# Two preparations of a two-block network: order of the weight splits around the running sums, and place of a narrow tanh

## The chip, the cores and the metric

One Trainium2 chip, one core. The metric is the device time of one execution in microseconds (us), as the median of several executions.

## The reference

The reference runs two blocks one behind the other on 256 tokens of width 1024, in float32. The first block has two layers of hybrid attention with an MLP and is not touched by the change. The second block has two layers, too, each of the form below. What matters here is the third branch, a recurrence of the RWKV-7 kind.

```python
h = rms_norm_2(x, norm_g) * (1.0 + scale) + shift
proj = h @ w_in      # pool, retention and rwkv branches, gates
...
p = p + (p_prev - p) * shift_mu                  # the mix
r, wl, k, v, al = jnp.split(p, split_pts, axis=-1)
w = -jax.nn.softplus(-(w0 + jnp.tanh(wl) @ w2)) - 0.5
decay = jnp.exp(-jnp.exp(w))
a = jax.nn.sigmoid(a0 + al @ a2)
kk = heads(k * k_k)
kk = kk / jnp.maximum(jnp.sqrt(jnp.sum(kk * kk, -1, keepdims=True)), 1e-12)
k = k * (1.0 + (a - 1.0) * k_a)
...
S = S * w_t + sa * b_t + v_t * k_t               # step by step over the tokens
```

The kernel does the recurrence in chunks of 128 tokens, so it needs the logarithms of the decays, summed along the tokens ("running sums"), and their exponentials.

## The kernel before, in words

**Engines.** The program of each engine is written out by hand, in order: `tensor_program`, `vector_program`, `scalar_program`, `gpsimd_program` and `sync_program` (which issues the loads). They meet through one semaphore per engine: `at["name", l]` is the step of VectorE, ScalarE or GpSimd that a waiting engine needs in layer `l`, and `done[...]` a step of TensorE. An engine that waits holds up all that stands behind in its program.

**Weight pieces.** The weights come in pieces of 128 x 2048 float32 (1 MB), in the order of the list `SECOND`: rw6 (half as wide), rw0 to rw5, rq0, rq1, rk0, rk1, u0, u1, rv0, rv1, rg0 and so on. The load of piece n waits until the low half of piece n - 3 has been made (ring of three). ScalarE rounds a piece to its high part in two instructions (`split_to`, printed under L2290, "part0h<-ring"; the piece before must be finished on TensorE but one, as there are two sets of parts). VectorE then makes the low part, raw minus high, in two instructions (L1284, "part0l<-ring,part0h"); GpSimd does so for some other pieces. TensorE multiplies each piece in three products (high x high, high x low, low x high), 48 instructions of 256 columns (L532). Pieces alternate between part0 and part1: rq1, rk1, u1 and rv1 use the same set in one layer, rq0, rk0, u0 and rv0 the other.

**Jobs.** `Jobs.fill()` takes the next job off a list that is the same for every engine: rq0, rq1, rk0, rk1, u0, u1, rv0, rv1, rg0, ... On TensorE a job multiplies its piece. On VectorE the job of a piece splits the low part of the piece after it (`use` goes one ahead), so the job rk1 on VectorE is the split of u0. On ScalarE it splits the high part of the next piece, then copies the job's own result out of PSUM ("Z<-ps"), which waits for the last product. On GpSimd the job rk1 also runs `rotate` (L2882 to L2888), 24 instructions: the rotation of rq, which waits for the copies of rq0 and rq1, then that of rk, which waits for those of rk0 and rk1.

**The stage.** `prepare(l, jobs)` opens each layer. TensorE multiplies rw6 and rw0 to rw5; each is copied out by ScalarE into `praw` and mixed by VectorE (L2009, L2013). Then TensorE goes on in this order:

```python
        jobs.fill()                  # rq0
        ...                          # lw, aa: 8 products "ps<-Z,v2b", need tanh(wa)
        for _ in range(4):
            jobs.fill()              # rq1, rk0, rk1, u0
        ...                          # ksum: 4 products "ps<-kt_,cg", need M.kt = bt ** 2
        jobs.fill()                  # u1
        ...                          # kn: products of the key norms, need n8
        jobs.fill()                  # rv0
        jobs.fill()                  # rv1
        ...                          # transposes of v4, then of bt and kt
```

Around this, ScalarE takes the tanh of `wa` (64 x 256, the narrow one), of `lw` and `aa`; VectorE scales `lw` (L2019), forms the running sums `cu` in eight instructions (L2024), the sum `sS` and the middle values (L2029 to L2032), subtracts them (L2035, step "cm"), multiplies r by the exponential that ScalarE makes of it (L2039, "ar r", waits for "e+"), and scales the keys into `bt` (L2042, step "kk"). ScalarE squares these into `kt` ("kk2"), which TensorE sums over each head ("ksum"). Then come the maximum, root and reciprocal of the norms (L2045, L2048), the difference of the running sums (L2051), and the products into AR, bt and kt (L2055 to L2068), the last of which waits for GpSimd's update of k4 (L2930, L2933).

The change touches `prepare` of `vector_program` and `prepare` of `scalar_program`. Tiles are printed by their buffers: gates is lw, cu, r4, k4 and others; bt_ is bt; kt_ is kt; sc is sS and the middle values; Z holds wa, ee, n8, and the copies of rq, rk, u and rv.

Of the kernel before, what the change touches and what calls it, by code (L numbers as in the profile page):

```python
# [11 lines left out]
ACT = mybir.ActivationFunctionType  # L12
# [65 lines left out]
PIECE = {(l, key): n for n, (l, key, width) in enumerate(PLAN)}  # L78
# [370 lines left out]
def jobs2():  # L449

    names = [f"{n}{j}" for n in ("rq", "rk", "u", "rv", "rg", "pg", "wg") for j in range(2)]
    first = [[n] for n in names]
    halves = [f"h{b}_{j}.{m}" for b in range(3) for j in range(4) for m in range(2)]
    bw = [f"bw{b}_{hf}.{m}" for b in range(2) for hf in range(2) for m in range(2)]
    first += [halves[0:2]] + [[n] for n in halves[2:14]] + [halves[14:16]]
    return first + [halves[16:18]] + [[n] for n in halves[18:24] + ["pr"] + bw[0:5]] + [bw[5:7], bw[7:8]]
# [812 lines left out]
def vector_program(w, K):  # L1269
    e, M, V, ps, at, done = w.e, K.mem, K.vector, K.psum, K.at, K.done  # L1270
# [722 lines left out]
    def prepare(l, jobs):  # L1993
        Z = M.Z[l]
# [26 lines left out]
        for c in range(4):  # L2021
            for i in range(2):
                n_ = slice(i * 128, (i + 1) * 128)
                e.tensor_tensor_scan(cu[:, c, n_], ui[:, 128:256], lw[:, c, n_], 0.0, ALU.mult, ALU.add).then_inc(*V())  # L2024
        jobs.fill()
        cu8 = cu.rearrange("p c (i n) -> p c i n", i=2)
        sS, mid = sc2[:, 36:40], sc2[:, 40:48]
        w.wait_ge(*V.now())
# [4 lines left out]
        w.wait_ge(*V.now())  # L2033
        cu_f = cu.rearrange("p c (i n) -> p (c i) n", i=2)
        e.tensor_tensor(cu_f, cu_f, mid.unsqueeze(2).to_broadcast([128, 8, 128]), ALU.subtract).then_inc(*V("cm", l))  # L2035
        ar_a, ar_r = M.AR[:, :, :, 0, :], M.AR[:, :, :, 1, :]
        spl = lambda t: t.rearrange("p c (i n) -> p c i n", i=2)
        w.wait_ge(*at["e+", l])
        e.tensor_tensor(ar_r, spl(r4), spl(ee), ALU.mult).then_inc(*V("ar r", l))  # L2039
        jobs.fill()  # L2040
        for c in range(4):
            e.tensor_scalar(bt[:, c, :], k4[:, c, :], second_vectors(l, "kk")[:, c:c + 1], None, ALU.mult).then_inc(*V("kk", l))  # L2042
        jobs.fill()
# [2 lines left out]
        ps.free(("ksum", l), V.now())  # L2046
        w.wait_ge(*at["n8 root", l])
        e.reciprocal(Z.n8, Z.n8).then_inc(*V("n8", l))  # L2048
        jobs.fill()
        w.wait_ge(*V.now())  # L2050
        e.tensor_tensor(lw, cu, lw, ALU.subtract).then_inc(*V("lw in", l))  # L2051
        for cp in range(2):
# [59 lines left out]
        for cp in range(2):  # L2112
            t = bank("yT", cp, l)
            for m in range(2):
                c = 2 * cp + m
# [133 lines left out]
    for l in range(L):  # L2249
        jobs = Jobs(jobs2(), lambda name: job2(l, name))  # L2250
# [30 lines left out]
def scalar_program(w, K):  # L2281
    e, M, S, ps, at, done = w.e, K.mem, K.scalar, K.psum, K.at, K.done
# [3 lines left out]
    def act(o, a, f, **k):  # L2286
        return e.activation(o, a, f, **k)  # L2287

    def copy(o, a):
        return e.activation(o, a, ACT.Copy)  # L2290

    def split_to(n):
        while state["split"] <= min(n, len(PLAN) - 1):
            m = state["split"]
            state["split"] += 1
            raw, hi, c = K.raw(m), K.part(m)[0], PLAN[m][2] // 2
            w.wait_ge(*at["piece", m])
            if m >= SPLIT:
                w.wait_ge(*done["piece", m - SPLIT])
            for h in range(2):  # L2300
                copy(hi[:, h * c:h * c + c], raw[:, h * c:h * c + c]).then_inc(*S("hi", m, h))
# [282 lines left out]
    def enter(b):  # L2584

        split_to(PIECE[b, "rw6"])
        squares(b, 0)
        scale_rows(b, 0)
        split_to(PIECE[b, "rw0"])
        modulate(b, 0)  # L2590
        squares(b, 1)
        high_of(b, 0, 0)
        scale_rows(b, 1)
        high_of(b, 0, 1)
        modulate(b, 1)
        for q in range(2):
            high_of(b, 1, q)
# [46 lines left out]
    def prepare(l, jobs):  # L2644
        Z = M.Z[l]
        S.mark("s", "begin", l)
        enter(l)
        c_ = M.cst[:, l, :]
        begins("begin", l)
        mixed = ("mixed", -1, l)  # L2650
        for j in (6, 0, 1, 2, 3, 4, 5):
            nch = 2 if j < 6 else 1
            use(l, f"rw{j}")
            t = bank(("rw", j), l)
            w.wait_ge(*at[mixed])
            copy(Z.praw[:, 0:nch, 1:257], v(t[:, :], c=2, n=256)[:, 0:nch, :]).then_inc(*S("praw", j, l))
            ps.free((("rw", j), l), S.now())
            mixed = ("mix", j, l)
        jobs.fill()
        w.wait_ge(*at["mix", 6, l])  # L2660
        act(Z.wa[0:64, :], Z.wa[0:64, :], ACT.Tanh).then_inc(*S("wl", l))
        for cp in range(2):
            for n, dst, hb in (("lw", M.lw, c_[:, 24:28]), ("aa", M.aa, c_[:, 28:32])):
                t = bank(n, cp, l)
                for m in range(2):
                    c = 2 * cp + m
                    act(dst[:, c, :], t[:, m * 256:(m + 1) * 256], ACT.Tanh, scale=0.5, bias=hb[:, c:c + 1]).then_inc(
                        *S("tanh " + n, cp, l))
                ps.free((n, cp, l), S.now())
        jobs.fill()  # L2670
        jobs.fill()
        sS, ee = M.sc2[:, 36:40], Z.ee
        w.wait_ge(*at["sS in", l])
        act(sS, sS, ACT.Exp).then_inc(*S("sS", l))
        w.wait_ge(*at["cm", l])
        act(ee, M.cu, ACT.Exp).then_inc(*S("e+", l))
        jobs.fill()
        w.wait_ge(*at["kk", l])
        act(M.kt, M.bt, ACT.Square).then_inc(*S("kk2", l))
        jobs.fill()  # L2680
        w.wait_ge(*at["n8 in", l])
        act(Z.n8, Z.n8, ACT.Sqrt).then_inc(*S("n8 root", l))
        jobs.fill()
        w.wait_ge(*at["lw in", l])
        act(M.lw, M.lw, ACT.Exp).then_inc(*S("e lw", l))
        jobs.fill()
        w.wait_ge(*at["ar r", l])
        act(ee, M.cu, ACT.Exp, scale=-1.0).then_inc(*S("e-", l))
        jobs.fill()
        S.mark("s", "ph2", l)  # L2690
        for i in range(2):
            copy(M.vN[:, i, :], bank("vN", i, l)[:, :]).then_inc(*S("vN", i, l))
            ps.free(("vN", i, l), S.now())
        for n, dst in (("bN", M.bN), ("kN", M.kN)):
            copy(dst, bank(n, l)[:, :]).then_inc(*S(n, l))
            ps.free((n, l), S.now())
        jobs.fill()
        jobs.need("u1")
        begins("ph2", l)
        copy(Z.dT[:, 0:2, :], v(bank("pool", 0, l)[:, :], c=2, n=256)).then_inc(*S("dT", 0, l))  # L2700
        ps.free(("pool", 0, l), S.now())
        for i in range(2):
            copy(Z.qTr[:, :, i * 128:(i + 1) * 128], v(bank("qT", i, l)[:, :], h=4, n=128)).then_inc(*S("qT", i, l))
            ps.free(("qT", i, l), S.now())
        jobs.fill()
        jobs.fill()
        w.wait_ge(*at["rot", l])
        for hf in range(2):
            copy(M.grow[:, hf * 512:(hf + 1) * 512], bank("grow", hf, l)[:, :]).then_inc(*S("grow", l))
            ps.free(("grow", hf, l), S.now())  # L2710
        jobs.need("rv1")
        jobs.fill()
        jobs.fill()
        jobs.need("rg0", "rg1", "pg0", "pg1")
        S.mark("s", "ph3", l)
# [6 lines left out]
    for l in range(L):  # L2722
        lnw = V2N * l + V2O["lnw"][0]
        jobs = Jobs(jobs2(), lambda name: job2(l, name))
# [551 lines left out]
```

## Time and profile before

| | |
|---|---|
| median of 3 runs | 1742.17 us (1741.64 to 1742.19) |
| profiled execution, its own time | 1739.01 us |
| its span, first to last instruction | 1737.2 us |
| mean granted TensorE clock | 0.993 |
| busy: TensorE / VectorE / ScalarE / GpSimd | 96% / 58% / 41% / 36% |
| preparation up to the transposes of bt and kt, layer 0 | 1011.8 to 1110.9 us |
| the same stretch of layer 1 | 1378.9 to about 1476 us |

All durations in the document come from one profiled execution, 1739.01 us long, of which the span is 1737.2 us; the runs without a profile took some 3 us more. "Idle before" in a row of the timeline is the time that the engine stood still ahead of the instruction, with the engine and line that released it. A matmul's printed duration (0.28 us) is longer than its share of the time, as matmuls overlap; starts of successive ones are 0.12 us apart at the full clock of 2.4 GHz.

### The profile page before, as it was taken

To read this page: it belongs to the slowest core of one execution; us is meant where nothing else is said; L and a number is where in the kernel's file an instruction comes from. 1 tells how busy PE (TensorE), PEld (TensorE's weight loads), DVE (VectorE), ACT (ScalarE), POOL (GpSimd) and SP (SyncE) were. 2 spreads that over 40 slices of the span, in tenths; PEclk is the share of its full clock that TensorE was granted. 3 is DMA by queue.
4 is the path that set the end of the run, shared out by engine and by line. 5 is a ranking of instruction groups with operands and counts; after the bars stand their busy time and mean duration, and the time that the engine had idled before them with its cause. 6 is when DMAs were issued, how large, how long until landed. Compare 5 with 4: busy or idle time off the path is not lost.

```text
span 1737.2 us, 34448 instructions
## 1 busy us (share of the span) xinstructions
PE 1673.1 (96%) x15214; PEld 1534.2 (88%) x15214; DVE 1008.5 (58%) x1612; ACT 718.8 (41%) x1120; POOL 628.0 (36%) x510
## 2 busy tenths in 40 slices
PE   9999999999999999999999998999999999999997
PEld 8878988899988888987999888999998898999986
DVE  4265366777763454476777876663345668653346
ACT  4434534545344444444444444533222444332223
POOL 1744683000307635733000414225544207144541
PEclk9999999999999999999999999999999999999999
DMA  8422444777545323465775544433223444432322
GB/s 344 148 81 90 137 162 201 274 283 265 178 173 187 123 75 118 142 258 202 271 279 201 175 170 146 159 122 123 99 98 122 144 154 146 153 123 98 123 74 109
DMA packets 44148, 283.57 MB, mean 163 GB/s; under 512 B 5160, under 2 KB 5288, under 8 KB 14176
## 3 DMA queue, kind: packets, MB, share of 16 engines
q1 hardware_dynamic: 42336, 272.23, 44.1%
q0 software_dynamic: 1664, 9.15, 1.4%
q8 instruction: 119, 1.95, 0.5%
q14 instruction: 29, 0.24, 0.0%
HBM read 280.30 MB, written 1.06 MB: 162 GB/s over the span
## 4 chain that ended last, share of the span: by engine, by line
PE 81%; DVE 9%; POOL 5%; ACT 4%; issue 1%; DMA 0%; SPq 0%; POOLq 0%; ACTq 0%; DVEq 0%
PE ps L532 78%; PE ps L540 2%; POOL part0l L2765 2%; POOL part1l L2765 2%; ACT Xh L2290 1%; DVE Xl L1299 1%; DVE part1l L1284 1%; DVE gates L2024 1%; DVE part0l L1284 1%; ACT part1h L2290 1%; ACT part0h L2290 0%; DMA hid<-in_xT 0%; ACT gates L2287 0%; POOL x L2800 0%; ACT raw L2287 0%
## 5 line engine op out<-in xcount | busy, mean ns | idle before, releaser
L2290 ACT ACTIVATE part0h<-ring 128x1024 fp32r<-128x1024 f32 (+2 forms) x218 | 216.3, 1041 | 264.2 <-PE ps L532 256.9
L532 PE MATMUL ps<-Xh,part0h 128*128 128x256 f32 x1080 | 314.9, 292 | 6.0 <-DVE Xl L1299 4.2
L2290 ACT ACTIVATE part1h<-ring 128x1024 fp32r<-128x1024 f32 x218 | 216.3, 1040 | 238.4 <-PE ps L532 236.8
L532 PE MATMUL ps<-Xl,part0h 128*128 128x256 f32 x1080 | 307.5, 285 | 0.0
L532 PE MATMUL ps<-Xh,part0l 128*128 128x256 f32 x1080 | 307.3, 285 | 0.0
L532 PE MATMUL ps<-Xh,part1h 128*128 128x256 f32 x984 | 285.2, 290 | 3.0 <-DVE Xl L1932 1.8
L2765 POOL TENSOR_TENSOR part1l<-ring,part1h 128x512 fp32r<-128x512 f32 x178 | 231.7, 1335 | 152.4 <-ACT part1h L2290 152.4
L2765 POOL TENSOR_TENSOR part0l<-ring,part0h 128x512 fp32r<-128x512 f32 x170 | 224.7, 1355 | 167.8 <-ACT part0h L2290 167.8
L532 PE MATMUL ps<-Xl,part1h 128*128 128x256 f32 x984 | 278.7, 283 | 0.0
L532 PE MATMUL ps<-Xh,part1l 128*128 128x256 f32 x984 | 278.5, 283 | 0.0
L532 PEld LDWEIGHTS ps<-Xh,part0h 128*128 128x128 f32 x1080 | 208.8, 193 | 15.8 <-issue 6.3
L532 PEld LDWEIGHTS ps<-Xl,part0h 128*128 128x128 f32 x1080 | 208.8, 193 | 0.3
L532 PEld LDWEIGHTS ps<-Xh,part0l 128*128 128x128 f32 x1080 | 208.9, 193 | 0.0
L1284 DVE TENSOR_TENSOR part0l<-ring,part0h 128x1024 fp32r<-128x1024 f32 (+1 forms) x132 | 165.9, 1296 | 62.5 <-ACT part0h L2290 62.2
L532 PEld LDWEIGHTS ps<-Xh,part1h 128*128 128x128 f32 x984 | 188.9, 192 | 10.2 <-issue 6.3
L1284 DVE TENSOR_TENSOR part1l<-ring,part1h 128x1024 fp32r<-128x1024 f32 x128 | 155.2, 1254 | 62.0 <-ACT part1h L2290 62.0
L532 PEld LDWEIGHTS ps<-Xl,part1h 128*128 128x128 f32 x984 | 189.0, 192 | 0.1
L532 PEld LDWEIGHTS ps<-Xh,part1l 128*128 128x128 f32 x984 | 188.9, 192 | 0.0
L2800 POOL TENSOR_TENSOR x<-xh,rows 128x512 f32<-128x512 f32 x20 | 33.5, 1673 | 335.8 <-DVE hid L1811 290.8
L532 PE MATMUL ps<-part1h,Xh 128*128 128x256 f32 (+2 forms) x304 | 95.7, 315 | 8.1 <-DVE part1l L1284 3.9
L532 PE MATMUL ps<-Z 64*64 64x64 f32 (+2 forms) x2256 | 98.5, 224 | 0.0
L532 PEld LDWEIGHTS ps<-Z 64*64 64x64 f32 (+1 forms) x2256 | 88.8, 136 | 8.0 <-issue 1.0
(410 smaller groups left out, 3319.2 us busy)
## 6 DMA issues: line engine op xcount, KB each, us to landing
ring<-in_w SPq DMA_DIRECT2D x214, 1024.0 KB, 4.9
hid<-in_ada SPq DMA_DIRECT2D x36, 512.0 KB, 6.5
hid<-in_w SPq DMA_DIRECT2D x6, 1024.0 KB, 11.0
rows<-in_lnrow POOLq DMA_DIRECT2D x6, 1024.0 KB, 7.2
fqk<-in_ada SPq DMA_DIRECT2D x6, 512.0 KB, 6.1
cq<-in_ada SPq DMA_DIRECT2D x6, 512.0 KB, 6.2
gates<-in_c SPq DMA_DIRECT2D x2, 1536.0 KB, 6.4
plain<-in_w SPq DMA_DIRECT2D x2, 1024.0 KB, 7.6
```

What stands on the lines that cost most here:

```text
L532: return e.matmul(o, a, b, start=st, stop=sp)
L540: return e.transpose(o, a, ident[0:a.shape[0], 0:a.shape[0]])
L1284: e.tensor_tensor(lo[:, h * c:h * c + c], raw[:, h * c:h * c + c], f32(hi[:, h * c:h * c + c]), ALU.subtract).then_inc(*V("low", m, h))
L1299: return e.tensor_tensor(hl[1], raw, f32(hl[0]), ALU.subtract).then_inc(*V(*name))
L2024: e.tensor_tensor_scan(cu[:, c, n_], ui[:, 128:256], lw[:, c, n_], 0.0, ALU.mult, ALU.add).then_inc(*V())
L2290: return e.activation(o, a, ACT.Copy)
L2765: e.tensor_tensor(lo[:, o], raw[:, o], f32(hi[:, o]), ALU.subtract).then_inc(*G("low", m, h))
L2800: e.tensor_tensor(x3[:, i, c], xh3[:, i, c], M.rows[:, c], ALU.mult).then_inc(*G())
```

## The change

- VectorE's job rk0 (the split of rk1) moves into the loop of running sums, behind the fourth of the eight; another job, rk1 (the split of u0), stands behind the eighth.
- VectorE's next job, u0 (the split of u1), stands behind the subtraction L2035 and ahead of the wait for "e+". The jobs that stood behind "ar r" and behind the reciprocal are gone; that behind the key scaling is now u1 (the split of rv0). The job behind "ar a" is rv0, as before.
- ScalarE takes the narrow tanh in the loop over the wide pieces, behind the copy of rw1 (j == 1), and no longer behind the job rq0.
- ScalarE does three jobs (rq1, rk0, rk1) ahead of the exponentials, and then the high half of u1. Behind the exponential of cu it does the job u0 and the high half of rv0, ahead of the squares. The squares, the root and the two other exponentials follow each other; the jobs u1, rv0 and rv1 come behind them.
- TensorE's, GpSimd's and the load program are unchanged, and so is what is computed.

```diff
--- before.py
+++ after.py
@@ -2022,7 +2022,8 @@
             for i in range(2):
                 n_ = slice(i * 128, (i + 1) * 128)
                 e.tensor_tensor_scan(cu[:, c, n_], ui[:, 128:256], lw[:, c, n_], 0.0, ALU.mult, ALU.add).then_inc(*V())
-        jobs.fill()
+            if c % 2:
+                jobs.fill()
         cu8 = cu.rearrange("p c (i n) -> p c i n", i=2)
         sS, mid = sc2[:, 36:40], sc2[:, 40:48]
         w.wait_ge(*V.now())
@@ -2033,11 +2034,11 @@
         w.wait_ge(*V.now())
         cu_f = cu.rearrange("p c (i n) -> p (c i) n", i=2)
         e.tensor_tensor(cu_f, cu_f, mid.unsqueeze(2).to_broadcast([128, 8, 128]), ALU.subtract).then_inc(*V("cm", l))
+        jobs.fill()
         ar_a, ar_r = M.AR[:, :, :, 0, :], M.AR[:, :, :, 1, :]
         spl = lambda t: t.rearrange("p c (i n) -> p c i n", i=2)
         w.wait_ge(*at["e+", l])
         e.tensor_tensor(ar_r, spl(r4), spl(ee), ALU.mult).then_inc(*V("ar r", l))
-        jobs.fill()
         for c in range(4):
             e.tensor_scalar(bt[:, c, :], k4[:, c, :], second_vectors(l, "kk")[:, c:c + 1], None, ALU.mult).then_inc(*V("kk", l))
         jobs.fill()
@@ -2046,7 +2047,6 @@
         ps.free(("ksum", l), V.now())
         w.wait_ge(*at["n8 root", l])
         e.reciprocal(Z.n8, Z.n8).then_inc(*V("n8", l))
-        jobs.fill()
         w.wait_ge(*V.now())
         e.tensor_tensor(lw, cu, lw, ALU.subtract).then_inc(*V("lw in", l))
         for cp in range(2):
@@ -2656,9 +2656,10 @@
             copy(Z.praw[:, 0:nch, 1:257], v(t[:, :], c=2, n=256)[:, 0:nch, :]).then_inc(*S("praw", j, l))
             ps.free((("rw", j), l), S.now())
             mixed = ("mix", j, l)
-        jobs.fill()
-        w.wait_ge(*at["mix", 6, l])
-        act(Z.wa[0:64, :], Z.wa[0:64, :], ACT.Tanh).then_inc(*S("wl", l))
+            if j == 1:
+                w.wait_ge(*at["mix", 6, l])
+                act(Z.wa[0:64, :], Z.wa[0:64, :], ACT.Tanh).then_inc(*S("wl", l))
+        jobs.fill()
         for cp in range(2):
             for n, dst, hb in (("lw", M.lw, c_[:, 24:28]), ("aa", M.aa, c_[:, 28:32])):
                 t = bank(n, cp, l)
@@ -2667,26 +2668,26 @@
                     act(dst[:, c, :], t[:, m * 256:(m + 1) * 256], ACT.Tanh, scale=0.5, bias=hb[:, c:c + 1]).then_inc(
                         *S("tanh " + n, cp, l))
                 ps.free((n, cp, l), S.now())
-        jobs.fill()
-        jobs.fill()
+        for _ in range(3):
+            jobs.fill()
+        split_to(PIECE[l, "u1"])
         sS, ee = M.sc2[:, 36:40], Z.ee
         w.wait_ge(*at["sS in", l])
         act(sS, sS, ACT.Exp).then_inc(*S("sS", l))
         w.wait_ge(*at["cm", l])
         act(ee, M.cu, ACT.Exp).then_inc(*S("e+", l))
         jobs.fill()
+        split_to(PIECE[l, "rv0"])
         w.wait_ge(*at["kk", l])
         act(M.kt, M.bt, ACT.Square).then_inc(*S("kk2", l))
-        jobs.fill()
         w.wait_ge(*at["n8 in", l])
         act(Z.n8, Z.n8, ACT.Sqrt).then_inc(*S("n8 root", l))
-        jobs.fill()
         w.wait_ge(*at["lw in", l])
         act(M.lw, M.lw, ACT.Exp).then_inc(*S("e lw", l))
-        jobs.fill()
         w.wait_ge(*at["ar r", l])
         act(ee, M.cu, ACT.Exp, scale=-1.0).then_inc(*S("e-", l))
-        jobs.fill()
+        for _ in range(3):
+            jobs.fill()
         S.mark("s", "ph2", l)
         for i in range(2):
             copy(M.vN[:, i, :], bank("vN", i, l)[:, :]).then_inc(*S("vN", i, l))
```

## Rows read from the trace of the kernel before

**Rows 1.** The page: busy time, share of the span and instructions of each engine.
```profile
PE 1673.1 (96%) x15214; PEld 1534.2 (88%) x15214; DVE 1008.5 (58%) x1612; ACT 718.8 (41%) x1120; POOL 628.0 (36%) x510
```

**Rows 2.** The page: chain that ended last, by engine.
```profile
PE 81%; DVE 9%; POOL 5%; ACT 4%; issue 1%; DMA 0%; SPq 0%; POOLq 0%; ACTq 0%; DVEq 0%
```

**Rows 3.** Timeline, TensorE, layer 0: start, duration, engine, line, operation, count, idle.
```profile
1011.82 0.36 PE L532 MATMUL ps<-Xh,part0h 128*128 128x256 f32 x1 [1.18 <-DVE Xl L1299]
...
1056.33 2.00 PE L532 MATMUL ps<-Z,v2b 64*128 64x256 f32 x16 [1.08 <-ACT Z L2287]
...
1071.84 0.39 PE L532 MATMUL ps<-part0h,Xh 128*128 128x256 f32 x1 [1.82 <-DVE part0l L1284]
...
1080.18 0.39 PE L532 MATMUL ps<-part1h,Xh 128*128 128x256 f32 x1 [2.10 <-DVE part1l L1284]
...
1087.59 1.89 PE L532 MATMUL ps<-kt_,cg 128*8 128x256 f32 x8
...
1110.86 0.22 PE L532 MATMUL ps<-cg,bt_ 64*64 64x64 f32 x1
```

**Rows 4.** Timeline, TensorE, layer 1.
```profile
1378.93 0.35 PE L532 MATMUL ps<-Xh,part1h 128*128 128x256 f32 x1 [1.19 <-DVE Xl L1299]
...
1438.91 0.38 PE L532 MATMUL ps<-part1h,Xh 128*128 128x256 f32 x1 [1.80 <-DVE part1l L1284]
...
1447.23 0.39 PE L532 MATMUL ps<-part0h,Xh 128*128 128x256 f32 x1 [0.82 <-DVE part0l L1284]
...
1453.17 1.89 PE L532 MATMUL ps<-kt_,cg 128*8 128x256 f32 x8
```

**Rows 5.** Windows: stretch, sum, busy PE, PEld, DVE, ACT, POOL; granted clock, DMA share, GB/s.
```profile
582.50:586.00 3.50, 0.00 (x0) 0.00 (x0) 3.30 (x12) 0.67 (x2) 2.74 (x3) 1.00 0.23 37
...
586.50:590.00 3.50, 3.50 (x19) 3.37 (x18) 1.04 (x3) 2.13 (x10) 0.00 (x0) 0.52 0.55 232
...
1081.50:1085.00 3.50, 3.50 (x19) 3.50 (x18) 2.74 (x4) 0.73 (x1) 3.42 (x6) 0.51 0.79 243
```

**Rows 6.** Timeline, VectorE, layer 0.
```profile
1061.52 2.37 DVE L1284 TENSOR_TENSOR part1l<-ring,part1h 128x1024 fp32r<-128x1024 f32 x2 [7.47 <-ACT part1h L2290]
...
1064.53 5.66 DVE L2024 TENSOR_TENSOR_SCAN gates<-cg,gates 128x128 f32<-128x128 f32 x8
1070.11 3.35 DVE L1284 TENSOR_TENSOR part0l<-ring,part0h 128x1024 fp32r<-128x1024 f32 x2
...
1074.88 1.76 DVE L2035 TENSOR_TENSOR gates<-gates,sc 128x1024 f32<-128x1024 f32 x1
1077.77 1.23 DVE L2039 TENSOR_TENSOR AR<-gates,Z 128x1024 f32<-128x1024 f32 x1 [1.12 <-ACT Z L2287]
1078.91 2.35 DVE L1284 TENSOR_TENSOR part1l<-ring,part1h 128x1024 fp32r<-128x1024 f32 x2
1081.18 3.06 DVE L2042 TENSOR_SCALAR bt_<-gates,v 128x256 f32<-128x256 f32 x4
...
1109.07 1.23 DVE L2068 TENSOR_TENSOR kt_<-gates,Z 128x1024 f32<-128x1024 f32 x1 [2.95 <-POOL gates L2933]
...
1123.92 1.14 DVE L2082 TENSOR_SCALAR gates<-gates,v 128x256 f32<-128x256 f32 x4
```

**Rows 7.** Timeline, ScalarE, layer 0: the squares, a split, a copy out.
```profile
1084.27 1.06 ACT L2287 ACTIVATE kt_<-bt_ 128x1024 f32<-128x1024 f32 x1 [4.16 <-DVE bt_ L2042]
1085.24 1.99 ACT L2290 ACTIVATE part0h<-ring 128x1024 fp32r<-128x1024 f32 x2
1087.70 0.60 ACT L2290 ACTIVATE Z<-ps 128x512 f32<-128x512 f32 x1 [0.47 <-PE ps L532]
```

**Rows 8.** Timeline, GpSimd, layer 0: three instructions of the rotation.
```profile
1070.67 1.71 POOL L2884 TENSOR_TENSOR grow<-Z,cs 128x256 f32<-128x256 f32 x1
...
1080.24 1.62 POOL L2882 TENSOR_TENSOR grow<-Z,cs 128x256 f32<-128x256 f32 x1 [3.00 <-ACT Z L2290]
...
1091.27 0.73 POOL L2888 TENSOR_TENSOR Z<-grow 128x256 f32<-128x256 f32 x1
```

## The prediction

> **What bounds the kernel now.** I first read the busy times of the engines: TensorE is busy for 96% of the span and the next engine, VectorE, for 58% [rows 1]. The chain that ended last runs 81% on TensorE and 9% on VectorE [rows 2]. So a split, an exponential or a copy costs time only where TensorE stands and waits for it. I therefore read TensorE's own timeline in the second block's preparation, once for each layer, and looked for idle time ahead of an instruction. Layer 0 has three such places [rows 3]: 1.08 us ahead of the small products of the decay weights (released by the narrow tanh on ScalarE), 1.82 us ahead of rk1 and 2.10 us ahead of u0 (both released by the low half that VectorE splits off). Layer 1 has 1.08 us at the first place too (its row repeats that of layer 0), then 1.80 us ahead of rk1 and 0.82 us ahead of u0 [rows 4]. After these waits the granted clock falls to half: 0.51 over 3.5 us in layer 0 [rows 5]. What that costs is seen on the piece in which it falls. An undisturbed piece runs from 1447.23 to 1453.17, 5.94 us [rows 4]; u0 in layer 0 took 1080.18 to 1087.59, 7.41 us [rows 3]; rk1 in layer 1 took 1438.91 to 1447.23 - 0.82 = 1446.41, 7.50 us [rows 4]. That is 1.5 us lost in each layer. All that the change could win here is 2 x 1.08 + 1.82 + 2.10 + 1.80 + 0.82 + 2 x 1.5 = 11.7 us.
>
> Next I followed what TensorE needs right behind u0: the key sums ("ksum", the products of kt_). They need the squares on ScalarE, these need the four scalings of the keys on VectorE (L2042), and these stand behind everything that VectorE does from the split of rk0 on. VectorE's timeline [rows 6] shows this run from 1061.52 to 1081.18 + 3.06 = 1084.24, 22.72 us with one gap of 1.12 us (for the first exponential). The squares follow at 1084.27, for 1.06 us [rows 7]. The key sums began at 1087.59 in layer 0, only 2.3 us after them. In layer 1 they began 1453.17 - 1378.93 = 74.24 us behind the layer's first wide product, against 1087.59 - 1011.82 = 75.77 us in layer 0 [rows 3, 4]; VectorE's run lies at the same distance in both layers, so there the squares were ready just 0.8 us before TensorE. **Two chains are nearly in step here: TensorE's pieces and VectorE's run to the key scaling. The change shortens the first by much and the second hardly.**
>
> **Part 1, the narrow tanh behind rw1.** It goes where ScalarE otherwise waits for TensorE, so it costs nothing there; its input is ready since the first mix. ScalarE's table stays the same, as no load stands before the tanh now. The products start when rq0 is done, 1055.30 instead of 1056.33: all behind them shifts by -1.03 us, in both layers.
>
> **Part 2, the split of rk1 between the two halves of the running sums.** The eight sums take 1070.11 - 1064.53 = 5.58 us [rows 6], so the split starts some 2.8 us earlier, at 1060.49 + (1064.53 - 1061.52) + 2.79 = 1066.3, and its first half is done by 1068.0. TensorE is free for rk1 at 1071.84 - 1.82 - 1.03 = 1069.0: the wait of 1.82 us (1.80) goes. The split of u0 comes right behind the other four sums, from 1072.4; its first half is ready at about 1074.1, and TensorE comes to it at 1074.8: the wait of 2.10 us (0.82) goes as well, with little to spare. TensorE is then through with u0 at about 1080.6 instead of 1087.6. ScalarE makes the high halves in time: it splits each piece right behind the copy of the one before.
>
> **Part 3, what VectorE does until the keys are scaled.** The run of 22.72 us keeps all its work. The gap of 1.12 us is filled by the split of u1, which is now ahead of the wait for the exponential: two instructions, 2.35 us when alone, 3.35 us beside GpSimd [rows 6]. GpSimd's rotation is why the second price matters. One of its instructions takes 1.71 us beside such a split and it starts on rk only when rk1 is copied out, at 1080.24 [rows 8]. rk1 is now copied at about 1075, so the rotation (12 instructions, about 12 us) runs on without a gap, across the split of u0, the split of u1, the product "ar r" and the key scaling. Before, u0's split (2.35) and "ar r" (1.23) had lain where GpSimd was idle. No row shows "ar r" beside GpSimd; the subtraction of the same size, L2035, took 1.76 us beside it, so "ar r" is bounded by 1.23 and 1.76. The key scaling already costs 3.06 us beside GpSimd, against 1.14 us for the same shape alone [rows 6]; it stays at 3.06. Low end: 22.72 - 1.12 + 2.35 = 23.95 us. High end: that + 1.0 (u1) + 1.0 (u0) + 0.53 = 26.48 us. I take 26.3, near the high end, because the rotation has no gap left. The keys are then scaled at 1060.49 + 26.3 = 1086.8, the squares are done at 1087.85, and the key sums start at about 1088.0 (1085.7 to 1088.2).
>
> The Trainium skill (SBUF — State Buffer, "Who interferes with whom") states that a VectorE instruction with two inputs in SBUF contends with a GpSimd instruction that reads SBUF. By it all three instructions pay and the sum is the high end; without it the sum is the low end, 2.5 us less in each layer. The trace agrees for the split (3.35 against 2.35 us), and the rule speaks against this change, which starts the rotation earlier.
>
> **Part 4, the split of rv0 ahead of the squares.** On ScalarE the copy of u0 (0.60 us) and the two splits of rv0 (1.99 us) now stand ahead of the squares [rows 7]. Both wait for u0's last product, at 1080.6, so they end near 1083.3. That is before the keys are scaled (1084.4 at the earliest), so they cost nothing; were VectorE faster, ScalarE would hold the key sums to 1083.3 + 1.06 + 0.15 = 1084.5. Behind the key sums nothing is late: VectorE has rv0's split done beforehand, and both later exponentials come earlier. The last operand of the transposes (kt_, done at 1109.07 + 1.23 = 1110.30, needed at 1110.86 [rows 3, 6]) follows the same chain from the key norms as before, and shifts with TensorE. The loads on SP's queue wait for low halves that come earlier or at most 2 us later, each some 10 us ahead of its use; no DMA is moved.
>
> **Part 5, the new wait and the clock.** TensorE now stands from 1080.6 to 1088.0, 7.4 us (5.1 to 7.6), ahead of the key sums. In this trace it stood idle over all of 582.50 to 586.00, and ran at a granted clock of 0.52 over 586.50 to 590.00 [rows 5]: 0.48 x 3.5 = 1.7 us lost. I expect the same here, 1.6 us in each layer, falling on the key sums and on u1. Bounds: nothing, as behind the wait of 1.82 us in layer 0 (rk1 then took 1080.18 - 2.10 - 1071.84 = 6.24 us, near the undisturbed piece); and 3.4 us, if two such stretches follow the longer wait.
>
> **Sum.** Layer 0: the key sums start at 1088.0 instead of 1087.6, +0.4, and 1.6 of clock behind them (the 1.5 before is already in 1087.59): +2.0. Layer 1: they start 1088.0 - 1011.82 = 76.2 us behind the first product instead of 74.24, +1.95, and 1.6: +3.55. Together +5.5 us on the profiled execution's 1739.0 us. That execution lies 3.2 us below the median shown; added to the median, 1742.2 + 5.5 = 1747.7 us.
>
> **Rivals.** (a) *The two chains come out even*: the splits and "ar r" find gaps in the rotation (low ends, -1.9 and -0.35), and the clock costs 0 to 1.6 once or twice: -2.2 to +1, 1740 to 1743. For it: the pieces of the rotation do not touch every split. Against it: 12 instructions without a gap, and clock losses after all but the shortest waits. (b) *Faster*: the rotation ends before the key scaling begins (before 1083.9), which then takes 1.14 instead of 3.06 us, and the clock does not fall: -2.2 - 2 x 1.9 = -6 us, 1736. It would need the rotation of rk done in 9 us from 1075, where it took 1091.27 + 0.73 - 1080.24 = 11.8 us [rows 8]. (c) *The plan works in full*: the squares are ready when u0 ends and all 11.7 us come back, 1730.5. It needs the keys scaled at 1079.4, 5 us before the low end. (d) *Slower by more*: two stretches at half clock in each layer, or kt_ passes its slack of 0.56 us: +8 to +9, 1751. (e) *It does nothing*: the high half of u1 must wait for rk1's last product; were it late, VectorE would only take its old gap at another place, within +-1 us of before. The high half is due at 1076.3, before VectorE asks at 1078.9.
>
> **Chances.** Forecast 0.62, (a) 0.18, (b) 0.04, (c) 0.01, (d) 0.11, (e) 0.04. About 0.2% (3.5 us) is what a measurement of this kernel can tell from no change. Slower by over that: 0.73; within: 0.22; faster: 0.05. The range takes in both ends of VectorE's run with one clock loss at the low end (-0.6), and both high ends with 2.5 us of clock a layer (+7.9), slightly widened: 1741.5 to 1750.5.
>
> **What would show it.** In the changed kernel's profile: no idle time ahead of the decay products, rk1 and u0; one long idle time ahead of the key sums, released by the squares on ScalarE, 5 to 7.6 us, in both layers; u1's split at 3.3 us beside GpSimd; a granted clock near 0.5 while u1 starts, and none near 0.5 in rk1 or u0. The forecast is wrong if the wait ahead of the key sums is under 4 us, or if the key scaling takes under 2 us.

## The result and the profile after

The changed kernel takes 1749.91 us as the median of 4 runs (1747.60 to 1751.51), the kernel before 1741.95 us in the same series; the ratio is 1.0046, with a 95% interval of 1.0032 to 1.0059. So the change made it slower, by 8.0 us between the medians. The forecast was 1747.7 us, with a range of 1741.5 to 1750.5. The profiled execution of the changed kernel took 1749.85 us, near its median, whereas the one before (1739.01 us) lies 3 us below its own; the two profiles are 10.8 us apart.

To see where these lie I cut both traces at the same instructions of TensorE: the first wide product of a layer (the rows 1011.82 and 1378.93 before) and the first product of rg0, right behind the transposes of bt and kt. I call the part between them **the stretch**; all that the change touches lies in it. First the windows of the changed kernel, then those of the kernel before; columns as in [rows 5], the busy times in the order PE, PEld, DVE, ACT, POOL.

```profile
1014.91:1117.97 103.06, 95.74 (x864) 91.21 (x864) 70.34 (x77) 46.96 (x62) 35.21 (x32) 0.97 0.48 162
1385.61:1489.25 103.64, 96.34 (x864) 91.78 (x864) 70.33 (x77) 46.94 (x62) 34.69 (x31) 0.95 0.45 156
1117.97:1385.61 267.64, 259.85 (x3097) 243.93 (x3093) 131.67 (x260) 86.25 (x117) 107.58 (x84) 0.99 0.34 116
```

```profile
1011.82:1112.83 101.01, 96.01 (x865) 92.41 (x865) 67.64 (x77) 46.88 (x62) 31.28 (x32) 0.98 0.48 164
1378.93:1478.40 99.47, 95.77 (x864) 92.37 (x864) 67.77 (x77) 46.78 (x62) 33.32 (x31) 0.98 0.47 161
1112.83:1378.93 266.10, 258.35 (x3096) 242.44 (x3093) 131.59 (x260) 86.16 (x117) 107.62 (x84) 1.00 0.34 117
```

The stretch is 2.05 us longer in layer 0 and 4.17 us longer in layer 1, 6.2 us together. The rest of the 10.8 us lies in code that does not differ: 3.09 us ahead of the first stretch (1014.91 against 1011.82) and 1.54 us between the two. Nearly all of it is TensorE taking longer over the same products. Its busy time grew by 2.6 us in the first part and by 1.5 us in the second (259.85 against 258.35), and in both the clock was at half for longer. Over the same early stretch of the kernel, and over one between the layers where the changed kernel has a half-clock spell, the windows show (changed, then before):

```profile
12.00:20.00 8.00, 8.00 (x44) 8.00 (x44) 3.33 (x8) 5.25 (x8) 1.52 (x5) 0.57 1.01 395
...
1294.00:1300.00 6.00, 4.66 (x28) 4.53 (x30) 4.91 (x9) 0.68 (x1) 0.11 (x1) 0.72 0.52 175
```

```profile
12.00:20.00 8.00, 8.00 (x57) 8.00 (x57) 3.85 (x9) 6.05 (x9) 1.52 (x5) 0.79 1.01 395
...
1288.00:1300.00 12.00, 10.23 (x175) 9.82 (x169) 7.22 (x13) 1.53 (x2) 0.96 (x1) 1.00 0.24 89
```

The spell between the layers follows a wait of the same length in both kernels (changed, then before); only the changed one has half clock around it:

```profile
1295.34 0.36 PE L532 MATMUL ps<-Xh,part1h 128*128 128x256 f32 x1 [1.78 <-DVE Xl L1932]
```

```profile
1290.18 0.36 PE L532 MATMUL ps<-Xh,part1h 128*128 128x256 f32 x1 [1.77 <-DVE Xl L1932]
```

Inside the stretch, TensorE's timeline of the changed kernel answers to [rows 3] and [rows 4]:

```profile
1014.91 0.36 PE L532 MATMUL ps<-Xh,part0h 128*128 128x256 f32 x1 [1.18 <-DVE Xl L1299]
...
1058.26 0.92 PE L532 MATMUL ps<-Z,v2b 64*128 64x256 f32 x6
...
1090.80 0.59 PE L532 MATMUL ps<-kt_,cg 128*8 128x256 f32 x1 [7.32 <-ACT kt_ L2287]
...
1100.52 0.86 PE L532 MATMUL ps<-Z,cg 8*64 8x256 f32 x5
...
1461.47 1.01 PE L532 MATMUL ps<-kt_,cg 128*8 128x256 f32 x2 [7.30 <-ACT kt_ L2287]
...
1471.80 1.08 PE L532 MATMUL ps<-Z,cg 8*64 8x256 f32 x8
```

The decay products start 43.35 us behind the first wide product (44.51 before) without a wait, and no idle time is left ahead of rk1 and u0. In their place stands one wait of 7.3 us ahead of the key sums, released by the squares. VectorE's timeline, which answers to [rows 6], shows what the squares wait for:

```profile
1063.47 2.37 DVE L1284 TENSOR_TENSOR part1l<-ring,part1h 128x1024 fp32r<-128x1024 f32 x2 [6.35 <-ACT part1h L2290]
1065.77 0.68 DVE L2019 TENSOR_SCALAR gates<-gates 128x1024 f32<-128x1024 f32 x1
1066.48 2.38 DVE L2024 TENSOR_TENSOR_SCAN gates<-cg,gates 128x128 f32<-128x128 f32 x4
1068.79 3.38 DVE L1284 TENSOR_TENSOR part0l<-ring,part0h 128x1024 fp32r<-128x1024 f32 x2
1072.09 3.42 DVE L2024 TENSOR_TENSOR_SCAN gates<-cg,gates 128x128 f32<-128x128 f32 x4
1075.42 3.38 DVE L1284 TENSOR_TENSOR part1l<-ring,part1h 128x1024 fp32r<-128x1024 f32 x2
...
1080.24 1.23 DVE L2036 TENSOR_TENSOR gates<-gates,sc 128x1024 f32<-128x1024 f32 x1
1081.39 3.44 DVE L1284 TENSOR_TENSOR part0l<-ring,part0h 128x1024 fp32r<-128x1024 f32 x2
1084.75 1.75 DVE L2041 TENSOR_TENSOR AR<-gates,Z 128x1024 f32<-128x1024 f32 x1
1086.41 3.15 DVE L2043 TENSOR_SCALAR bt_<-gates,v 128x256 f32<-128x256 f32 x4
```

VectorE works without a gap from 1063.47 to 1086.41 + 3.15 = 1089.56: 26.1 us instead of 22.7. All three splits take 3.4 us and "ar r" 1.75 us. GpSimd's rotation lies beside it from 1066.92 on: 24 instructions up to 1094.97 with one gap of 0.17 us, ahead of the first instruction on rk.

```profile
1080.28 1.79 POOL L2883 TENSOR_TENSOR grow<-Z,cs 128x256 f32<-128x256 f32 x1 [0.17 <-ACT part0h L2290]
...
1094.24 0.73 POOL L2889 TENSOR_TENSOR Z<-grow 128x256 f32<-128x256 f32 x1
```

The clock around the wait is in the windows of the changed kernel:

```profile
1083.50:1087.00 3.50, 0.00 (x0) 0.00 (x0) 3.50 (x3) 2.49 (x3) 3.50 (x3) 1.00 0.33 66
1087.00:1090.50 3.50, 0.00 (x0) 0.00 (x0) 3.50 (x5) 0.90 (x1) 3.34 (x6) 0.66 0.56 234
1090.50:1094.00 3.50, 3.20 (x8) 0.95 (x8) 2.39 (x2) 1.44 (x2) 3.42 (x3) 0.50 0.08 9
1094.00:1097.50 3.50, 3.50 (x25) 3.20 (x25) 2.57 (x3) 1.70 (x2) 0.96 (x2) 0.87 0.77 290
```

It falls while TensorE still stands and stays at half through the key sums. From the key sums to the key norms the changed kernel takes 1100.52 - 1090.80 = 9.72 us in layer 0 and 1471.80 - 1461.47 = 10.33 us in layer 1; before it was 1095.37 - 1087.59 = 7.78 us, at full clock.

### The profile page after: what moved, and what is told of

It is laid out like the page before. It is cut to its first block, busy times and chain, and to the rows that moved or that the text cites. A ratio compares the mean times of both kernels' runs of the same rounds, so it can differ in the third digit from the quotient of the medians.

```text
span 1748.1 us, 34454 instructions
## 1 busy us (share of the span) xinstructions
PE 1677.4 (96%) x15214; PEld 1536.4 (88%) x15214; DVE 1014.1 (58%) x1612; ACT 719.9 (41%) x1120; POOL 633.3 (36%) x510
## 4 chain that ended last, share of the span: by engine, by line
PE 80%; DVE 9%; POOL 5%; ACT 4%; issue 1%; DMA 0%; SPq 0%; POOLq 0%; ACTq 0%; DVEq 0%
PE ps L532 78%; PE ps L540 2%; POOL part0l L2766 2%; POOL part1l L2766 2%; DVE part1l L1284 1%; DVE part0l L1284 1%; ACT Xh L2290 1%; DVE Xl L1299 1%; DVE gates L2024 1%; ACT part1h L2290 1%; ACT part0h L2290 0%; DMA hid<-in_xT 0%; DVE bt_ L2043 0%; ACT gates L2287 0%; POOL x L2801 0%
```

## The experiments

Eleven kernels ran, all beside the kernel before. The table gives the start of the key sums behind the layer's first wide product (layer 0; layer 1 agrees within 0.1 us in every kernel but the one before, where it is 74.2), the stretch in both layers, and the whole time. The stretches are read from one profiled execution of each kernel. Ratios are to the kernel before on the same chip and are not exactly the quotients of the medians. The medians of the kernel before were 1741.27 us (e1 to e4), 1740.92 us (e5, e6, e9, e7) and 1740.37 us (e10 to e12).

| kernel | key sums | stretch, layers 0 and 1 | median | ratio (95% interval) |
|---|---|---|---|---|
| before | 75.8 | 101.0, 99.5 | 1741.95 | 1 |
| changed | 75.9 | 103.1, 103.6 | 1749.91 | 1.0046 (1.0032 to 1.0059) |
| e12 changed again | 75.9 | 103.1, 103.7 | 1749.71 | 1.0044 (1.0028 to 1.0059) |
| e1 unread products in the wait | 75.8 | 101.0, 101.0 | 1743.54 | 1.0016 (1.0007 to 1.0026) |
| e2 u1 split behind the keys | 73.2 | 100.0, 100.7 | 1745.02 | 1.0024 (1.0014 to 1.0034) |
| e3 squares first | 75.9 | 102.9, 103.6 | 1748.90 | 1.0045 (1.0030 to 1.0060) |
| e4 rotation after keys | 72.2 | 103.6, 103.3 | 1751.08 | 1.0056 (1.0040 to 1.0073) |
| e10 rk's rotation after keys | 72.3 | 99.1, 98.8 | 1739.09 | 0.9988 (0.9978 to 0.9997) |
| e5 tanh alone | 73.2 | 98.4, 98.4 | 1738.97 | 0.9989 (0.9979 to 0.9998) |
| e7 keys early, old splits | 73.2 | 98.4, 98.4 | 1738.52 | 0.9987 (0.9977 to 0.9997) |
| e6 keys early | 68.5 | 96.5, 96.5 | 1733.81 | 0.9964 (0.9952 to 0.9975) |
| e9 keys early, norms first | 68.5 | 95.9, 95.9 | 1733.32 | 0.9955 (0.9938 to 0.9971) |
| e11 e9, rk's rotation after ar r | 68.5 | 96.2, 97.4 | 1738.03 | 0.9980 (0.9971 to 0.9990) |

### What the wait costs beyond itself: e1_dummies_in_wait

```diff
         t = ps.take(w, "ksum", l)
+        keep_busy(14)                 # products that nobody reads
         w.wait_ge(*at["kk2", l])
```

> The changed kernel with 14 unread products of TensorE (0.43 us each, 6.0 us) in the wait ahead of the key sums, of 7.3 us. My theory: the wait lets the clock fall to half, and the key sums and the start of u1 pay for it (in the changed kernel key sums to key norms take 9.7 us in layer 0 and 10.3 in layer 1, against 7.8 before). Then they take 7.8 us in both layers here, the key sums start when they did (75.9 us behind the layer's first wide product), and the time falls by 4 to 5 us. Rival (the wait is all of the loss, the clock belongs to the rest of the kernel): key sums to key norms stay at 9.7 to 10.3 us and the time stays.

TensorE's timeline of this kernel, in which the 14 unread products are 28 instructions:

```profile
1082.70 6.21 PE L532 MATMUL ps<-cg 128*128 128x256 f32 x28
...
1090.08 1.89 PE L532 MATMUL ps<-kt_,cg 128*8 128x256 f32 x8 [1.17 <-ACT kt_ L2288]
...
1097.86 1.94 PE L532 MATMUL ps<-Z,cg 8*64 8x256 f32 x16
```

The key sums start when they did (75.8 us) and the next step comes after 7.78 us, in both layers. The stretch is shorter by 2.03 us and 2.65 us, 4.7 us in all, of which 4.5 us are the half clock (9.72 and 10.33 against 7.78). Each against the kernel before in its own series, the medians differ by 5.7 us; beside the 4.7 us, the part between the layers is back at 266.1 us, as before. So the half clock behind the wait is worth some 4.5 of the 6.2 us, and it comes from the idle time itself. Work without use, put into a wait, gets it back.

### Which engine holds the squares: e2_u1_split_behind_keys and e3_squares_first

e2, on VectorE:

```diff
         e.tensor_tensor(cu_f, cu_f, mid..., ALU.subtract).then_inc(*V("cm", l))
-        jobs.fill()
...
             e.tensor_scalar(bt[:, c, :], k4[:, c, :], ...).then_inc(*V("kk", l))
         jobs.fill()
+        jobs.fill()
```

> The changed kernel, but VectorE splits the low half of u1 behind the key scaling instead of ahead of the wait for the exponential. My theory (VectorE's run sets the key sums): the run loses the split (3.4 us) and regains the gap of 1.1 us, so the key sums start 2.3 us earlier, 73.6 us behind the first wide product, in each layer; the time falls by about 4.6 us, if as much clock is lost. Rival (ScalarE's order sets them: copy of u0, split of rv0, squares): they start where they did, 75.9 us, and the time stays.

e3, on ScalarE:

```diff
         act(ee, M.cu, ACT.Exp).then_inc(*S("e+", l))
-        jobs.fill()
-        split_to(PIECE[l, "rv0"])
         w.wait_ge(*at["kk", l])
         act(M.kt, M.bt, ACT.Square).then_inc(*S("kk2", l))
+        jobs.fill()
+        split_to(PIECE[l, "rv0"])
```

> The changed kernel, but ScalarE takes the squares ahead of the job u0 and of the high half of rv0. My theory (VectorE's run sets the key sums): nothing moves, the key sums start 75.9 us behind the first wide product, within 0.3 us, and the time stays within 1 us; the low half of rv0 may come some 3 us later, hidden by u1. Rival (the jobs put ahead of the squares cause the wait): the wait of 7.3 us shrinks to under 4 us and the time falls by 6 us or more.

In e2 the key sums start at 1089.49 - 1016.31 = 73.2 us, 2.7 us earlier (2.3 expected), the wait is 4.6 us, and the stretch is shorter by 3.0 us in each layer. VectorE's rows of e2 show why: the gap is back, and "ar r" is cheap again, which I had not counted.

```profile
1083.99 1.26 DVE L2040 TENSOR_TENSOR AR<-gates,Z 128x1024 f32<-128x1024 f32 x1 [1.13 <-ACT Z L2287]
1085.17 3.08 DVE L2042 TENSOR_SCALAR bt_<-gates,v 128x256 f32<-128x256 f32 x4
1088.18 2.88 DVE L1284 TENSOR_TENSOR part0l<-ring,part0h 128x1024 fp32r<-128x1024 f32 x2
```

In e3 nothing moves: the key sums at 75.9 us, the wait 7.3 us, the stretch within 0.2 us. ScalarE, with its jobs out of the way, just stands for 7.01 us ahead of the squares:

```profile
1087.44 1.06 ACT L2287 ACTIVATE kt_<-bt_ 128x1024 f32<-128x1024 f32 x1 [7.01 <-DVE bt_ L2043]
```

Together they show that VectorE's run up to the key scaling sets the key sums, and that ScalarE's jobs ahead of the squares cost nothing there.

### What makes VectorE's run long: e4_rotation_after_keys and e10_rk_rotation_after_keys

In GpSimd's `rotate`, e4 adds the first wait, e10 the second one instead:

```diff
         w.wait_ge(*at["cs"])
+        w.wait_ge(*at["kk", l])           # e4: the whole rotation
         for src, n in ((Z.rq3, "rq"), (Z.rk3, "rk")):
+            if n == "rk":
+                w.wait_ge(*at["kk", l])   # e10: rk only
```

> The changed kernel, but GpSimd's rotation waits until the keys are scaled. My theory (VectorE's run is long because GpSimd works beside it): the splits of rk1, u0 and u1 take 2.35 instead of 3.4 us, the key scaling 1.15 instead of 3.1, the sums and ar r a little less, in all about 6 us; the keys are then scaled near 67.5 us behind the first wide product and ScalarE's order (copy of u0, split of rv0) sets the key sums, at about 72.4 us; wait 3.8 us, time 6 to 9 us lower. Rival (the run is long by VectorE's own work): less than 1.5 us of it goes, the wait stays above 6 us, and the time stays.

> The changed kernel, but only the second half of GpSimd's rotation, that of rk, waits until the keys are scaled; that of rq stays where it is. My theory (VectorE's run is long because GpSimd works beside it; e4_rotation_after_keys lost what it gained only because the whole rotation then ran into the update of k4): the split of u1, ar r and the key scaling take 2.35, 1.2 and 1.15 us, the run is 3.5 us shorter, the key sums start 72.3 us behind the first wide product, the rotation ends some 10 us before the update of k4, kt_ is in time, and the stretch from the first wide product to rg0 takes 99.5 to 100.5 us (103.1 and 103.6 in the changed kernel). Rival (the order of GpSimd's work is a zero sum here): the wait comes back at kt_, and the stretch takes 102.5 us or more.

In e4 VectorE's run, from the split of rk0 to the scaled keys, takes 1081.91 + 1.14 - 1062.61 = 20.4 us instead of 26.1, and it now holds two gaps, 2.12 and 1.66 us, that wait for ScalarE's high halves; so its work is just 16.7 us. GpSimd stands for 20.35 us meanwhile. These rows of e4 stand against those of the changed kernel above:

```profile
1066.98 2.36 DVE L1284 TENSOR_TENSOR part0l<-ring,part0h 128x1024 fp32r<-128x1024 f32 x2
1069.26 1.36 DVE L2024 TENSOR_TENSOR_SCAN gates<-cg,gates 128x128 f32<-128x128 f32 x4
1072.74 2.36 DVE L1284 TENSOR_TENSOR part1l<-ring,part1h 128x1024 fp32r<-128x1024 f32 x2 [2.12 <-ACT part1h L2290]
1075.13 0.17 DVE L2030 TENSOR_TENSOR sc<-gates 128x4 f32<-128x4 f32 x1
...
1078.50 2.36 DVE L1284 TENSOR_TENSOR part0l<-ring,part0h 128x1024 fp32r<-128x1024 f32 x2 [1.66 <-ACT part0h L2290]
1080.78 1.22 DVE L2041 TENSOR_TENSOR AR<-gates,Z 128x1024 f32<-128x1024 f32 x1
1081.91 1.14 DVE L2043 TENSOR_SCALAR bt_<-gates,v 128x256 f32<-128x256 f32 x4
...
1083.13 0.72 POOL L2884 TENSOR_TENSOR grow<-Z,cs 128x256 f32<-128x256 f32 x1 [20.35 <-DVE bt_ L2043]
```

The key sums start at 72.2 us, as expected; here ScalarE's order sets them, as its squares follow the split of rv0 without a gap. Yet the time is no lower, and the expectation missed: the rotation now ends at 1108.4, GpSimd's update of k4 stands behind it, and TensorE waits 3.16 us for kt_ (2.33 us in layer 1), with half clock behind it: from the key norms to rg0 it takes 22.2 and 20.9 us instead of 17.5.

```profile
1114.38 0.24 PE L532 MATMUL ps<-cg,bt_ 64*64 64x64 f32 x1 [3.16 <-DVE kt_ L2068]
...
1107.70 0.74 POOL L2890 TENSOR_TENSOR Z<-grow 128x256 f32<-128x256 f32 x1
1108.43 2.16 POOL L2932 TENSOR_SCALAR gates<-gates,v,cst 128x256 f32<-128x256 f32 x4
```

I had not asked what is queued behind the rotation. e10 does: only rk's half waits. VectorE's run takes 22.5 us, with the split of u1, "ar r" and the key scaling at 2.35, 1.22 and 1.13 us, the key sums start at 72.3 us, there is no wait for kt_, and the stretch is 99.1 and 98.8 us, slightly better than the 99.5 to 100.5 expected. The rotation ends 6.5 us before the update of k4, not 10. One added wait on GpSimd turns the changed kernel from 0.44% slower into 0.12% faster than before.

### The parts one at a time: e5_tanh_alone and e7_keys_early_old_splits

e5 is the kernel before with the tanh moved as the change does it. e7 has this, and the key scaling and the squares moved early (diff below), with the splits where they were.

> The kernel before, with the narrow tanh moved behind the copy of rw1 and nothing else. My theory: the 1.08 us ahead of the decay products go and all behind them shifts by 1.03 us, as VectorE's run starts earlier by the same; the stretch from the first wide product to rg0 takes 100.0 us in layer 0 and 98.4 us in layer 1 (101.0 and 99.5 before), the waits ahead of rk1 and u0 stay at 1.8 and 0.8 to 2.1 us, and the time falls by 2 us. Rival (ScalarE's copy of rq0 holds the decay products anyway, or the shift is lost in the next wait): the stretch stays within 0.3 us.

> The kernel before with the tanh and the key scaling and squares moved early, but the weight splits where they were. My theory: the waits ahead of rk1 and u0 (1.8 and 2.1 us, with 1.5 us of clock) stay, because the splits set them, so the stretch is that of e5_tanh_alone within 1 us, 99 to 100 us; moving the splits only pays together with the early keys. Rival (the key scaling is what the splits were late for): the waits fall under 1 us and the stretch is that of e6_keys_early.

e5 gains more than expected in layer 0: 2.6 us, not 1.0; in layer 1 it is the 1.05 us. Its waits ahead of rk1 and u0 are 1.91 and 0.84 us in layer 0, not 1.82 and 2.10:

```profile
1073.25 0.36 PE L532 MATMUL ps<-part0h,Xh 128*128 128x256 f32 x1 [1.91 <-DVE part0l L1284]
...
1081.57 0.36 PE L532 MATMUL ps<-part1h,Xh 128*128 128x256 f32 x1 [0.84 <-DVE part1l L1284]
```

The half clock fell in rk1 here (7.5 us for the piece) and in u0 before: when rk1 runs slowly, TensorE reaches the wait ahead of u0 later and the wait hides most of it. The kernel before shows the same within one execution: 101.0 us in layer 0, with the spell in u0, and 99.5 us in layer 1, with the spell in rk1. Why the spell falls in one piece or the other is not settled, and only one execution of the kernel before was profiled, so 1.5 of the 2.6 us may belong to that execution; the whole time of e5 fell by 0.02% to 0.21%, which can't tell. e7 gives the same stretch as e5 to 0.02 us (99 to 100 us expected): without the moved splits the early keys are worth nothing.

### A version that beats both: e6, e9 and e11

The key scaling needs only k4, mixed since rw3. e6 puts it where VectorE stood for 6.35 us:

```diff
         jobs.fill()
+        w.wait_ge(*V.now())
+        for c in range(4):
+            e.tensor_scalar(bt[:, c, :], k4[:, c, :], ...).then_inc(*V("kk", l))
         jobs.fill()
         after(("tanh lw", 1, l))
...                                  # and, on ScalarE, behind the job rq1:
+        w.wait_ge(*at["kk", l])
+        act(M.kt, M.bt, ACT.Square).then_inc(*S("kk2", l))
```

The same lines are taken out at their old places. e9 also moves one `jobs.fill()` of VectorE from ahead of the maximum to behind the reciprocal; e11 adds to e9 a wait of rk's rotation for "ar r".

> The changed kernel, with the key scaling on VectorE right behind the mixes, where it waits for ScalarE, and the squares on ScalarE behind the job rq1: the inputs are there since the mix of rw3. My theory (two chains in step, of which the change shortened one): the wait of 7.3 us ahead of the key sums goes, no half clock in the stage; the key norms then wait about 2 us and the transposes of kt_ about 1 us, and the stretch from the first wide product to rg0 takes 97 us in both layers (101.0 and 99.5 before, 103.1 and 103.6 changed); the time falls by about 12 us against the changed kernel and by 6 us against before. Rival (what VectorE has to do up to kt_ sets the stretch, in whatever order): it takes 101 us or more, with the wait at the transposes.

> As e6_keys_early, and VectorE takes the maximum and the reciprocal of the norms ahead of the low half of rv0, not behind it. My theory: the wait of 2 us ahead of the key norms goes, and kt_ comes as early as TensorE asks for it: the stretch takes 94.5 to 95.5 us, and the time is 4 us below e6_keys_early. Rival (GpSimd's update of k4 behind its rotation holds kt_): the wait moves to the transposes, and the stretch stays at 97 us.

> As e9_keys_early_norms_first, and the rotation of rk waits for ar r. My theory: the split of u1 and ar r are 1.5 us shorter, but the 12 instructions then lie beside the split of rv0, the difference, the products into bt and the split of rv1, all of which are on the way to kt_: what is gained comes back, and the stretch stays within 0.7 us of 95.9 us, with 1 to 2.5 us of wait for kt_. Rival (contention ahead of the norms is what makes kt_ late): the wait for kt_ goes and the stretch takes 94.2 us.

In e6 the wait ahead of the key sums is gone. What is left is 1.2 us ahead of the key norms, with a half-clock spell behind it that I had not expected (granted clock 0.78 over 1092 to 1096), and the stretch is 96.5 us. In e9 that wait is gone, too; one of 1.8 us for kt_ takes its place, and the stretch is 95.9 us, longer than the 94.5 to 95.5 expected. The clock stayed full:

```profile
1014.23:1110.14 95.91, 94.12 (x865) 90.79 (x865) 69.07 (x77) 46.66 (x62) 39.45 (x32) 1.00 0.49 170
1377.69:1473.59 95.90, 94.11 (x865) 90.78 (x865) 69.07 (x77) 46.66 (x62) 38.98 (x31) 1.00 0.48 165
```

The reciprocal of the norms was done 2.9 us earlier than in e6, but the split of rv0 now lay between it and the difference of the running sums, and kt_ was ready 0.8 us later than in e6. The rival of e9 (GpSimd holds kt_) did not hold either: GpSimd stood idle for 2.52 us ahead of its update. The chain to kt_ runs from the norms over VectorE, GpSimd and back to VectorE. In e11 the order against the rotation brought nothing: VectorE saved 1.6 us ahead of the norms and then stood 2.01 us for the root on ScalarE. Layer 0 stayed within 0.4 us of e9, as expected. Layer 1 lost 1.5 us and missed the expectation: 0.3 us of it is the longer wait for kt_ (2.11 against 1.79 us) and 1.2 us a half-clock spell behind it. I had expected e9 to be 4 us below e6. The stretches differ by 1.2 us in all, and which is the better can't be told from the whole times; both are some 7 us below the kernel before.

### The changed kernel again: e12_changed_again

> The changed kernel unaltered, on the same chip as the others and the kernel before, for the whole-kernel difference. My theory: the stretch costs 2.1 us in layer 0 and 4.2 us in layer 1 as in its profile, 6.2 us in all, and what the whole time differs by beyond that is half clock at other places, which varies from one execution to the next: the median lies 5 to 9 us above that of before. Rival (the change also costs something outside the stretch in every execution): 8 us or more again, and a further place in the trace that is longer by the same amount as in the first profile.

The stretch is the same to 0.06 us, and the median is 1749.71 against 1740.37 us, 9.3 us and not the 5 to 9 expected. The part between the layers is 267.6 us again, as in the first profile, with the half-clock spell at the same place, near 1296. So the second half of my expectation failed, and both signs of the rival came: 8 us or more, and a further place that is longer by the same amount. The other kernels fit it. All that have the moved splits show 267.4 to 267.8 us for this part (changed, e12, e2, e3, e4, e6, e9, e10, e11), with one exception, e1; this one, the kernel before, e5 and e7 show 266.1. So these 1.5 us go with the moved splits, e1 apart, though they lie outside the stretch. They come through the clock: no instruction there was moved, and the wait ahead of the spell is as long as before (1.78 against 1.77 us). Why the clock falls there in some kernels and not in others is not settled. The 3.09 us ahead of the first stretch are another matter: that part ends at 1011.8 in the profile of before and at 1012.8 to 1016.3 in all the others, whether or not they have the moved splits.

## Why the prediction was right

**The two chains in step** was right, and with it the sign. The waits ahead of the decay products, rk1 and u0 went, and TensorE then stood for the squares: 7.32 us measured, 7.4 forecast. e2 and e3 show that it was VectorE's run and not ScalarE's order.

**Part 1, the tanh**: 1.16 us instead of 1.03, and e5 shows the gain by itself.

**Part 3, the run**: 26.3 us forecast, 26.09 measured. The splits took 3.38, 3.38 and 3.44 us (3.35 taken) and "ar r" 1.75 us (1.23 to 1.76 given). That the high end was the right one to lean to is shown by e4: with GpSimd quiet the same instructions took 2.36 and 1.22 us, and the key scaling 1.14 us. One step of the reasoning was not quite so: the rotation of rk started at 1080.28, when that of rq was done, and not when rk1 was copied out; the split of u0 (1075.42 to 1078.80) paid for the rotation of rq. Another term fell out the other way: the subtraction L2036 took 1.23 us instead of the 1.76 us it had before. It started at 1080.24, just ahead of GpSimd's instruction at 1080.28, and there it was GpSimd's that took longer, 1.79 us instead of 0.74 us. Before, GpSimd's had started first.

The rule of the Trainium skill (SBUF — State Buffer, "Who interferes with whom") gave the high end, and the trace and e4 agree with it, scans and the 128x4 instructions included. It speaks of two inputs; the key scaling has one tensor as its input, and its 3.15 against 1.14 us is a measurement of this case.

**Part 4, rv0 ahead of the squares**: costed at nothing, and e3 shows nothing. The prediction also said where ScalarE's order would hold the key sums if VectorE were faster: 1084.5, which is 72.7 us behind the first wide product. e4 and e10 show 72.2.

**Part 5, the clock, was under-sized.** The step said 1.6 us in each layer; it was 1.94 us and 2.55 us (9.72 and 10.33 against 7.78). The row that I took it from follows an idle time of 3.9 us, after which the clock fell only once TensorE was at work again. Behind 7.3 us it had fallen before, and the key sums ran wholly at half.

**The sum.** Layer 0: +0.12 us for the start of the key sums and +1.94 us, 2.05 in all (2.0 forecast). Layer 1: 1461.47 - 1385.61 = 75.86 instead of 74.24, +1.62 us, and +2.55, 4.17 in all (3.55 forecast). Together 6.2 us against 5.5. Two errors partly cancel in it: the clock was 1.3 us more than forecast over both layers, and the key sums started 0.6 us less late. The +2.05 us of layer 0 also hangs on where the half clock fell in the profiled execution of before; with the spell in rk1, as in its layer 1, that stretch would have been some 1.5 us shorter and the change that much dearer.

The medians are 8.0 us apart, and 9.3 us in e12. Beyond the 6.2 us, 1.5 us are the spell between the layers, which no step of the prediction had: it followed the clock only inside the stretch. The nearness of 1747.7 to 1749.91 is thus in part luck, while the wait, its length and its cause are not.

**The rivals.** Even chains (a) fell with the three contended splits. (b) failed because the rotation ran until 1095, past the key scaling, which ended at 1089.6. (c) was out by VectorE's run. (d) is nearest in size for the clock of layer 1, but kt_ kept its slack: from the key norms to rg0 it takes 1117.97 - 1100.52 = 17.45 us, as before (17.46). (e) is out as well: u1's split starts at 1081.39 without a wait for its high half.

## What to carry to other kernels

Before a wait of the bounding engine is removed, find the next thing that engine will ask for and measure the slack of its chain. Here it was 2.3 us and 0.8 us, and in layer 0 5 us of removed waits turned into one of 7.3 us. The clock is part of a wait's price, also where the wait is short: 1.5 us a layer behind the waits of about 2 us, 1.9 and 2.6 us behind that of 7.3 us. The best cure was to start the chain where its inputs are ready (e6), and it paid only together with the moved splits (e7); a wait added to a third engine helps only if nothing urgent is queued behind it.

## What the runs showed of the hardware

- GpSimd beside VectorE: with the rotation out of the way, eight running sums took 1.37 + 1.36 us (e4), beside it 2.38 + 3.42 us (changed kernel); a 128x4 product took 0.17 instead of 0.59 us. I had counted the small ones and the sums as VectorE's own work.
- The granted clock fell to half during the 7.3 us wait and stayed there through the key sums behind it. 14 unread products in the wait kept it full (e1, 1.00 from 1082.7 to 1100).
- A wait behind a half-clock spell can hide its cost. In e5 the spell fell in rk1 and the next wait was 0.84 us instead of 2.10; the stretch was 1.5 us shorter, beyond the moved tanh, than with the spell in u0.
- The same wait, 1.77 to 1.78 us between the layers, was followed by half clock in nine profiles and by full clock in four (267.4 to 267.8 us and 266.1 us for that part).
